# One 128-row product per head instead of two 64-row products in the level stage of a chunked scan

## The reference, cut to what matters

```python
def rwkv7_scan(r, decay, k, v, a_vec, b_vec, s0, reverse):
    def step(S, inp):
        r_t, w_t, k_t, v_t, a_t, b_t = inp
        sa = jnp.einsum('bhij,bhj->bhi', S, a_t)
        S = S * w_t[:, :, None, :] + sa[..., None] * b_t[:, :, None, :] + v_t[..., None] * k_t[:, :, None, :]
        return S, jnp.einsum('bhij,bhj->bhi', S, r_t)
    ...
```

## Time and profile before

| What | Value |
|---|---|
| median of 3 runs | 3829.64 us (3829.46 to 3870.79) |
| profiled execution, its own time | 3845.05 us |
| profiled execution, span | 3843.3 us |
| PE busy | 3489.2 us, 91% of the span |
| PEld busy | 2955.5 us, 77% |
| DVE busy | 1812.8 us, 47% |
| ACT, POOL busy | 1183.0 us, 402.8 us |
| mean granted TensorE clock | 0.893 |

### The profile page before, as it was taken

How to read it: one execution, slowest core, us unless ns; L and a number is a source line. 1 busy time by engine, 2 the same in 40 slices (tenths; PEclk the granted TensorE clock), 3 DMA queues, 4 the chain that set the end, 5 groups by cost and what they waited for, 6 DMA issues and landing times. The chain is left out here.

```text
span 3843.3 us, 62413 instructions
## 1 busy us (share of the span) xinstructions
PE 3489.2 (91%) x27450; PEld 2955.5 (77%) x27450; DVE 1812.8 (47%) x2463; ACT 1183.0 (31%) x1648; POOL 402.8 (10%) x272
## 2 busy tenths in 40 slices
PE   5699998999999868989799998999776999999999
PEld 3487876899999747976599996777544788888887
DVE  5463545444444353226355553466342463636463
ACT  1444433221211132235544442353353211111111
POOL 0122221000000011221000002221011100000000
PEclk8799999666665579999899999999788999999999
DMA  8122233221211142132411102212111111111112
GB/s 332 47 95 88 81 121 113 68 68 36 68 35 41 52 153 99 45 127 80 170 49 61 55 19 110 86 52 80 61 44 66 50 47 50 45 51 48 51 48 73
DMA packets 145996, 294.54 MB, mean 77 GB/s; under 512 B 10048, under 2 KB 86976, under 8 KB 140224
## 3 DMA queue, kind: packets, MB, share of 16 engines
q1 hardware_dynamic: 126608, 212.95, 16.3%
q0 software_dynamic: 19120, 77.60, 6.0%
HBM read 211.22 MB, written 79.30 MB: 76 GB/s over the span
## 5 line engine op out<-in xcount | busy, mean ns | idle before, releaser
L60 PE MATMUL ev_ps<-h_hi,ev_w_hi 128*128 128x512 f32 (+1 forms) x792 | 289.0, 365 | 40.2 <-POOL ev_w_lo L360 38.9
L60 PE MATMUL ff_ps<-h_hi,ff_w_hi 128*128 128x512 f32 x768 | 300.1, 391 | 2.0 <-DVE ff_w_lo L3039 2.0
L61 PE MATMUL ff_ps<-h_lo,ff_w_hi 128*128 128x512 f32 x768 | 299.9, 390 | 0.0
L62 PE MATMUL ff_ps<-h_hi,ff_w_lo 128*128 128x512 f32 x768 | 299.7, 390 | 0.0
L61 PE MATMUL ev_ps<-h_lo,ev_w_hi 128*128 128x512 f32 (+1 forms) x792 | 281.4, 355 | 0.0
L62 PE MATMUL ev_ps<-h_hi,ev_w_lo 128*128 128x512 f32 (+1 forms) x792 | 281.3, 355 | 0.0
L3039 DVE TENSOR_TENSOR ff_w_lo<-ff_w,ff_w_hi 128x1024 fp32r<-128x1024 f32 (+1 forms) x80 | 89.5, 1119 | 339.6 <-ACT ff_w_hi L3014 339.6
L60 PEld LDWEIGHTS ev_ps<-h_hi,ev_w_hi 128*128 128x128 f32 x792 | 150.7, 190 | 79.9 <-POOL ev_w_lo L360 41.0
L3014 ACT ACTIVATE ff_w_hi<-ff_w 128x1024 fp32r<-128x1024 f32 (+1 forms) x80 | 78.0, 975 | 326.4 <-PE ff_ps L62 324.2
L60 PEld LDWEIGHTS ff_ps<-h_hi,ff_w_hi 128*128 128x128 f32 x768 | 144.9, 189 | 33.6 <-DVE ff_w_lo L3039 3.6
L62 PEld LDWEIGHTS ff_ps<-h_hi,ff_w_lo 128*128 128x128 f32 x768 | 144.9, 189 | 30.2
(11 more groups left out here) (501 smaller groups left out, 8605.5 us busy)
## 6 DMA issues: line engine op xcount, KB each, us to landing
ff_w<-in_w_up SPq DMA_DIRECT2D x48, 512.0 KB, 3.5
ev_w<-in_ev_w_in POOLq DMA_DIRECT2D x33, 512.0 KB, 3.9
ada_wt<-in_ada_w POOLq DMA_DIRECT2D x12, 1024.0 KB, 8.2
ada_wt<-in_ada_w SPq DMA_DIRECT2D x12, 1024.0 KB, 8.6
ff_w<-in_w_down SPq DMA_DIRECT2D x32, 384.0 KB, 3.0
ar<-ev_ar SPq DMA_DIRECT2D x8, 1280.0 KB, 5.4
bk<-ev_bk SPq DMA_DIRECT2D x8, 1280.0 KB, 8.0
sc_ar<-ar SPq DMA_DIRECT2D x20, 512.0 KB, 6.1
```

The costliest lines, as they stand in the source:

```text
L60: nc.tensor.matmul(out, w_hi, x_hi, start=start, stop=False)
L61: nc.tensor.matmul(out, w_hi, x_lo, start=False, stop=False)
L62: return nc.tensor.matmul(out, w_lo, x_hi, start=False, stop=stop)
```

## The change

The two 64x64 weight blocks of a head become one 128x128 weight block, with zeros in the two quadrants off the diagonal. Each of `level_p` and `level_z` makes 8 products per direction instead of 16. The right-hand operands X and Z and the results stay as they are. To make the wide weights, mD and Pm grow from 64 to 128 columns per head, their masks from two blocks of 32 columns to four, and a new mask `quarter` (made once on DVE, with two copies of pieces of `hm`) takes the place of `hm`. POOL now waits for that mask instead of the loaded constants.

```diff
--- before.py
+++ after.py
@@ -675,6 +675,7 @@
     ld = {(d, b): g.sem(f"sc_loaded{d}{b}") for d in range(2) for b in range(2)}
     yst = {(d, b): g.sem(f"sc_stored{d}{b}") for d in range(2) for b in range(2)}
     levels_ready = g.sem("sc_level_masks")
+    quarters = g.sem("sc_quarters")
     consts, zeroed = g.sem("sc_consts"), g.sem("sc_zeroed")
 
     def done(eng, x, d, n, r=None):
@@ -697,11 +698,11 @@
         mB, mK = sb("mB", [P, 2, 2, 8, 2, CH]), sb("mK", [P, 2, 2, 8, 2, CH])
         V, Bt, MV, Zf = sb("V", [P, 2, 2, BANK]), sb("Bt", [P, 2, 2, 2, BANK]), sb("MV", [P, 2, 2, BANK]), sb("Zf", [P, 2, 2, 8, CH])
         dg, Z, X, P5 = (sb(x, [P, 2, 8, 32]) for x in ("diag", "Z", "X", "P5"))
-        mD, Pm = sb("mD", [P, 2, 8, CH]), sb("Pm", [P, 2, 8, CH])
+        mD, Pm = sb("mD", [P, 2, 8, P]), sb("Pm", [P, 2, 8, P])
         W, U = sb("W", [P, 2, BANK]), sb("U", [P, 2, BANK])
         St, tmp, y = sb("S", [P, 2, 4, CH]), sb("Stmp", [P, 2, 4, CH]), sb("y", [P, 2, 2, 4, P])
         m1, mx = sb("m1", [P, 2, 2, CH]), sb("mx", [P, 2, 2, 32])
-        lmh = sb("lm_halves", [P, 2, NL, CH])
+        lmq, quarter = sb("lm_quarters", [P, 2, NL, P]), sb("quarter", [P, 2, CH])
         lm, hm, am, eye = sb("lm", [P, 2, NL, 32]), sb("hm", [P, CH]), sb("am", [P, 2]), sb("eye", [P, 32])
         bA, bB, bC, bD = ([ctx.enter_context(nc.psum_tensor(f"sc_b{x}{d}", [P, BANK], F32)) for d in range(2)] for x in "ABCD")
 
@@ -802,9 +803,7 @@
                             done(pe, "blocks", d, n)
                         settle()
                         for j in range(8):
-                            for q in range(2):
-                                c = half(q)
-                                last = mm(bA[d][c, 32 * j:32 * j + 32], mD[c, d, j], X[c, d, j], start=True, stop=True)
+                            last = mm(bA[d][:, 32 * j:32 * j + 32], mD[:, d, j], X[:, d, j], start=True, stop=True)
                         last.then_inc(S["P", d], 1)
 
                 def level_z(n, l):
@@ -814,9 +813,7 @@
                             done(pe, "MVev", d, n)
                         settle()
                         for j in range(8):
-                            for q in range(2):
-                                c = half(q)
-                                last = mm(bB[d][c, 32 * j:32 * j + 32], Pm[c, d, j], Z[c, d, j], start=True, stop=True)
+                            last = mm(bB[d][:, 32 * j:32 * j + 32], Pm[:, d, j], Z[:, d, j], start=True, stop=True)
                         last.then_inc(S["Z", d], 1)
 
                 def last_p(n):
@@ -935,14 +932,15 @@
 
             @block.gpsimd
             def _(pool):
-                pool.wait_ge(consts, 96)
+                pool.wait_ge(quarters, 3)
                 for n in range(NB):
                     for d in range(2):
                         done(pool, "mB", d, n)
                         if n:
                             done(pool, "P", d, n - 1, NL - 1)
-                        nc.gpsimd.tensor_tensor(mD[:, d], mB[:, n % 2, d, :, 0], hm[:].unsqueeze(1).broadcast_to([P, 8, CH]),
-                                                ALU.mult).then_inc(S["blocks", d], 1)
+                        nc.gpsimd.tensor_tensor(mD[:, d].rearrange("s j (q c) -> s j q c", q=2),
+                                                mB[:, n % 2, d, :, 0].unsqueeze(2).broadcast_to([P, 8, 2, CH]),
+                                                quarter[:].unsqueeze(1).broadcast_to([P, 8, 2, CH]), ALU.mult).then_inc(S["blocks", d], 1)
 
             @block.vector
             def _(dve):
@@ -971,9 +969,9 @@
                 def level_mask(n, l):
                     for d in range(2):
                         done(dve, "P", d, n, l)
-                        tt(Pm[:, d].rearrange("s j (a c) -> s j a c", a=2),
-                           bA[d][:, 0:256].rearrange("s (j c) -> s j c", j=8).unsqueeze(2).broadcast_to([P, 8, 2, 32]),
-                           lmh[:, d, l].rearrange("s (a c) -> s a c", a=2).unsqueeze(1).broadcast_to([P, 8, 2, 32]),
+                        tt(Pm[:, d].rearrange("s j (a c) -> s j a c", a=4),
+                           bA[d][:, 0:256].rearrange("s (j c) -> s j c", j=8).unsqueeze(2).broadcast_to([P, 8, 4, 32]),
+                           lmq[:, d, l].rearrange("s (a c) -> s a c", a=4).unsqueeze(1).broadcast_to([P, 8, 4, 32]),
                            ALU.mult).then_inc(S["Pm", d], 1)
 
                 def level_add(n, l):
@@ -1025,9 +1023,14 @@
 
                 nc.vector.memset(St[:], 0.0).then_inc(zeroed, 1)
                 dve.wait_ge(consts, 96)
+                nc.vector.memset(quarter[:], 0.0).then_inc(quarters, 1)
+                dve.wait_ge(quarters, 1)
+                for q in range(2):
+                    nc.vector.tensor_copy(quarter[half(q), q], hm[half(q)]).then_inc(quarters, 1)
+                dve.wait_ge(quarters, 3)
                 for d in range(2):
-                    tt(lmh[:, d].rearrange("s l (a c) -> s l a c", a=2), lm[:, d].unsqueeze(2).broadcast_to([P, NL, 2, 32]),
-                       hm[:].rearrange("s (a c) -> s a c", a=2).unsqueeze(1).broadcast_to([P, NL, 2, 32]), ALU.mult).then_inc(levels_ready, 1)
+                    tt(lmq[:, d].rearrange("s l (a c) -> s l a c", a=4), lm[:, d].unsqueeze(2).broadcast_to([P, NL, 4, 32]),
+                       quarter[:].rearrange("s q (a c) -> s (q a) c", a=2).unsqueeze(1).broadcast_to([P, NL, 4, 32]), ALU.mult).then_inc(levels_ready, 1)
                 dve.wait_ge(levels_ready, 2)
                 for n in range(NB + 1):
                     new, old = n < NB, n >= 1
```

## The result

| | before | after |
|---|---|---|
| median | 3834.68 us (3829.46 to 3870.79, 4 runs) | 4145.08 us (4136.18 to 4152.27, 4 runs) |
| profiled span | 3843.3 us | 4143.9 us |
| scan, first to last PE record | 650.3 us | 951.1 us |
| mean granted clock in the scan | 0.63 | 0.57 |

The ratio is 1.0786, with a 95% interval of 1.0726 to 1.0845: slower by 310 us between the medians and by 7.9% between the means, which the ratio compares. I forecast 4097 us, +267 us, and a range of 3925 to 4200. The direction and the main mechanism came out as written; the sum is 43 us short of the measured 310.

What follows compares the result with a forecast made beforehand. The prediction took PE, almost never waiting in the scan, as the bound. Ten iterations at +26.7 us (records 26.0, switches 0.7) plus 0.3 set-up made +267 on 3829.6: 4097 us, +7.0%, range 3925 to 4200.

Steps and rivals of the forecast that it cites:

- PE is the bound: In the scan, PE is busy 60.96 of 62.90 us, so each microsecond of PE work added or saved moves the end.
- A wide record costs its 128 weight columns: In level products, one 128-column record takes 0.112 us fast or 0.213 slow, twice the price of a 64x64 pair.
- half-price: Rival, chance 0.07: in level products a load costs half, 0.160 us slow and 0.085 fast per record; total 3960 us.
- hidden load: Rival, chance 0.05: in level products the next load runs beside the current record; only switches and set-up remain, about 3838 us.
- The work: In the scan, dearer level records add 26.0 us per iteration and shape switches 0.7; ten iterations plus 0.3 set-up give +267.
- The switches: Seven borders per iteration between products of two shapes, 0.1 us each: +0.7 us, from nothing up to 1.4.
- The clock's fall: In the level stage, the fall to 0.50 stays at about 938.8 us, after 18 fast records of Z0.
- The clock's rise: The rise comes ahead of the levels, in unchanged work; all iterations short or all long shifts the total -17 to +41 us.
- DVE, POOL and set-up cost nothing: DVE's longer mask (4 us per iteration) and POOL's mD (2.5 us) stay hidden; set-up adds 0.3 us once.
- The clock stays up: Rival, chance 0.05: wide level products keep the clock up through the iteration, 56.4 us each; total 3765 us, -1.7%.
- The rule on the clock: The skill's gate follows PE's busy time, which alone would give 3765 us; the trace disagrees, 60.96 of 62.9 us at 0.66.

## Why the prediction was right

- **PE is the bound.** Right. It has no wait in the ten blocks after the change. My reading of nine iterations was a little off: five, not six, take 61.4 to 62.9 us, and the ninth, 66.6 us at 0.65, holds the start of the next.
- **A wide record costs its 128 weight columns.** Right: 0.114 and 0.214 us against 0.112 and 0.213. The product with 64 columns on 128 rows and the repeats to 64 and 128 columns separate rows, weight columns and moving (right-hand) columns, and only the weight columns of one product move the price. The rivals with a half-price and a hidden load fall with it, and so does the Trainium skill's figure for one load (TensorE: Matmul & The Clock Gate, LDWEIGHTS), 107 ns for 128 columns, for products of this kind: the trace has 0.214 us per record at clock 0.50.
- **The work.** Right. The estimate from the table above, the scan with all of it at clock 0.50, grew by 253 us, where the sum had 267 for records and switches: too large by some 10 us, if at all. The switches cost a little more than I had: a 64-row record now starts 0.33 us after a wide one at clock 0.50, where a wide one follows after 0.21, and a wide one 0.24 us after a 64-row pair that takes 0.107. That is 0.12 or 0.13 for each of seven switches, 0.9 us per iteration, where I had 0.7.
- **The clock's fall.** This is the mis-sized term. The sum holds the fall where it was in time, 6.7 us behind the first record of P0, which puts the loss of fast time at nothing. In the iteration shown above, P0 begins at 1152.65 at 1.00, and Z0 at 1157.93 runs at 0.50 from its first record. I had 18 fast records there, 1.8 us. Over the scan, the time at 1.00 went from 174 to 126 us. Each of these 48 us costs 0.8 to 1 us, so the clock's part is some 40 to 48 us, and the sum had it at nothing. The scan shows a miss of only 34, because a slightly too large term for the work hides the rest.
- **The clock's rise.** The second part of it. The clock rises some 20 us into the iteration in seven of nine after the change, in three before, and about 8 or 9 us into it in the others. Averaged over the eight iterations between the second and the tenth start, an iteration went from 64.1 to 94.1 us, +30.0; my own range of 4050 to 4170 had allowed for all of them being long, with up to +41. Why the clock falls sooner and rises later isn't shown. The whole scan grew by 300.8 us, and the spans by 300.6. I counted 267. The rest of the 43 us between the medians, some 10, is how the profiled run of before stood to its median.
- **DVE, POOL and set-up cost nothing.** Right in that PE waits for none of them. In the experiment with the wide operands alone, where the bursts are short, PE waits 5 us more for DVE and the whole costs 21 us.
- **The clock stays up.** This rival (0.05) didn't happen, but the mechanism is real. With the clock up, the wide products take 3848 or 3858 us and the pairs 3747. At a low clock they take 4145 and 3845. So the doubled price of a record is worth 100 to 110 us at a high clock and 300 at a low one, and the low clock itself costs the pairs 98 us and the wide products some 290. The forecast took the low clock as given and priced only the records.
- **The rule on the clock.** The Trainium skill (TensorE: Matmul & The Clock Gate, Part 1: The HAM clock gate) lets the clock follow how busy PE is. The trace doesn't bear that out here: PE is busy 97 to nearly 100% of the scan at 0.63, at 0.57, at 0.85 and at 0.87, and only 93% of it in the kernel before with 64 right-hand columns, at 0.85. Busy time as the profile counts it doesn't tell these apart. What did raise the clock was more right-hand columns, or two products on all 128 rows in place of two on 64 each. The runs don't say what the chip goes by.

## What to carry to other kernels

Price a small 32-bit product with no more right-hand than weight columns by its weight columns: merging two that ran side by side into one of twice the width doubles its cost, even if the instruction count halves. Before cutting work on a PE that is always busy, look at its granted clock: where it is low, right-hand columns that cost no time (up to as many as weight columns) can be worth more than what one could save: here 2.5%, by repeating an operand. And a cover that holds in one version (a mask behind a long burst) has to be read again in the version with short bursts.

## What the runs showed of the hardware

- Repeating right-hand columns up to the number of weight columns left the distance of records alone at clock 1.00 (0.112 to 0.114 us for 32, 64 or 128 behind 128 weight columns; 0.027 to 0.029 for 32 or 64 behind 64) and raised the clock of the scan from 0.57 to 0.85 and from 0.63 to 0.85.
- Products with all 128 rows in common and separate halves of the columns run side by side, 0.058 us a pair at clock 1.00.
- Products of 32x32 on four separate pieces follow each other at 0.009 us per record at clock 1.00, but bursts of 64 records are interrupted by gaps in issue of up to 4.0 us.
- The same POOL product took 1.27 us for 512 elements and 2.33 for 1024, the DVE mask 0.69 and 1.22.
